# A two-layer encoder on one core: the memory branch loaded first, and the position bias made between the blocks of the first projection

## The chip, the cores and the metric

The kernel runs on one core of one Trainium2 chip. The metric is the device time of one execution in microseconds (us). The program drives TensorE (PE), VectorE (DVE), ScalarE (ACT) and GpSimd (POOL); SyncE (SP) issues every load on one queue.

## The reference, cut to what matters

256 tokens of width 1024 (`x`) and 256 memory rows of width 1024 (`mem`), all float32. Only the first stage is touched by the change; the rest (dense SwiGLU, a second layer with gated linear attention, top-2-of-8 experts, the final norm) follows it.

```python
mem_kv = rms_norm(mem, mem_norm) @ w_mem_kv          # 1024 -> 512: keys and values of 4 memory heads
u = rms_norm(x, even_norm1)
q, k, v, qm = split(u @ even_w_in)                   # 1024 -> 2560: 3 x 768 for 12 heads, 256 memory queries
mix = neighbourhood_attention(q, k, v, even_rpb)     # 12 heads, 4 x 64 grid, relative position bias, column mask
mo = softmax(qm @ mem_k.T / 8) @ mem_v               # 4 heads
h = x + concat([mix, mo]) @ even_w_out
...
```

## The kernel before

**Products in three parts.** Each float32 matrix product is made of three matmuls (`mul3`, L1288 to L1290) of a rounded high part and a low part: high by high, high by low, low by high. ACT makes the high part of each weight slot (`high_to`, L514), DVE the low part by subtraction (`low_to`, L849). A slot is 2048 columns (1 MB). `raw` holds 6 slots as loaded, `w_hi` and `w_lo` hold 3: the high part of slot n waits until the products of slot n-3 are done (`slot_done`), and the load of slot n waits until the low part of slot n-6 is made (`lo_ready`). Slots 0 and 1 are `w_mem_kv`; slots 2 to 11 are `even_w_in`, two for each block of 512 output columns (five blocks); a slot means 48 matmuls here, four output groups of twelve.

**A norm.** ACT squares and sums (`mean_squares`, L526), POOL makes 1/sqrt (L802, L805), DVE multiplies (`norm`, L864) into `xn`, PE transposes the 16 tiles (`turn`, L1309) into PSUM banks 0 to 3, and ACT and DVE cut these into `xt_hi` and `xt_lo` (`turned_high` L532, `turned_low` L870), four pieces each. `mem` is norm 0 and `x` is norm 1; both use the one buffer `gain` and the one pair `xt_hi`, `xt_lo`.

**The position bias.** `even_rpb` is loaded four times into `rp_a` at partitions 0, 32, 64 and 96 (31 rows each), two of the four shifted by one element (L418). DVE cuts it (L932, L933, L935), and 64 matmuls of 72 columns (`bias_products`, L1400) against slices of a shift matrix give, in ten groups of up to seven in banks 6 and 7, what DVE adds to a column mask (`bias_copy`, L924).

**The order by hand.** Each engine's program is written out; there is no planner. SP: tables, shifts, the four loads of the bias, `mem`, gain 0, slot 0, `x`, slots 1, 2 and 3, gain 1 (which waits until norm 0 is done), router and small tables, then the other slots. PE: bias groups 0 to 3, `turn(0)`, bias groups 4 and 5, slots 0 and 1, `turn(1)`, bias groups 6 to 9, slots 2 to 10, the scores of heads 0 and 1, slot 11, and then attention. Each block's four groups of 256 columns lie in four banks of their own, 0 to 3 and 4 to 7 in turn, and ACT (L587) and DVE (L971) copy two each.

Of the kernel before, what the change touches and what calls it, by code (L numbers as in the profile page):

```python
# [18 lines left out]
ALU = mybir.AluOpType  # L19
# [6 lines left out]
P = 128  # L26
# [103 lines left out]
def shape_constants(np):  # L130
# [13 lines left out]
    put("ident", (i == j) * 1.0)  # L144
    put("tri_f", (same & (i <= j)) / 16.0)
# [5 lines left out]
    c = np.arange(P) % GRID_W  # L151
    start = np.clip(c - 8, 0, GRID_W - 16)[:, None]
    cc = np.arange(GRID_W)[None, :]
    put("col_mask", np.where((cc >= start) & (cc < start + 16), 0.0, NEG))

# [16 lines left out]
def build(nc, col, tables, shifts, x, mem, gains, rpb, gate_aug, g_norm, router, mem_kv, even_in, even_out,  # L175
          even_gate, even_up, even_down, odd_in, odd_out, exp_gate, exp_up, exp_down, out):
    with ExitStack() as ctx:
# [18 lines left out]
        gain = sb("gain", [P, D])  # L196
        cst = sb("cst", [P, max(a + n for a, n in col.values())])
# [13 lines left out]
        rt_sb = states[:].rearrange("p d k n -> p (d k n)")[:, 0:KD * E].rearrange("p (k e) -> p k e", k=KD)  # L211
        arena = sb("arena", [P, ARENA])
# [15 lines left out]
        qkT = take(14 * T).rearrange("p (i t) -> p i t", t=T)  # L228
        v0 = take(TT * 768).rearrange("p (t n) -> p t n", t=TT)
        bias = take(NA_HEADS * NDR * GRID_W).rearrange("p (x c) -> p x c", c=GRID_W)  # L230
        s_a = take(3 * 2 * T).rearrange("p (b t m) -> p b t m", b=3, t=2)
        pT_a = take(2 * 2 * T).rearrange("p (b j q) -> p b j q", b=2, j=2)
        rp_a = take(NA_HEADS * RPB_R).rearrange("p (h r) -> p h r", r=RPB_R)
# [3 lines left out]
        mem_sb = arena[:, 0:TT * D].rearrange("p (t d) -> p t d", t=TT)  # L237
# [56 lines left out]
        def score_bank(i):  # L294

            return (0, 1, 6, 7)[i % 4] if i < 16 else 4 + i % 2
# [40 lines left out]
        def STATE_PS(d, k):  # L337
# [8 lines left out]
        tables_in, rpb_in, mem_in, x_in, gain_in = (  # L346
            sem("tables_in"), sem("rpb_in"), sem("mem_in"), sem("x_in"), sem("gain_in"))
# [47 lines left out]
        def _(sp):  # L395
# [23 lines left out]
            sp.dma_start(mem_sb, mem.rearrange("(t p) d -> p t d", p=P)).then_inc(mem_in, 16)
# [411 lines left out]
        def _(dve):  # L831
# [971 lines left out]
```

## Time and profile before

| | |
|---|---|
| median of 3 runs | 1532.38 us (1530.67 to 1533.03) |
| the profiled execution, time | 1531.72 us |
| the profiled execution, span of its instructions | 1529.9 us |
| PE, DVE, ACT busy | 96%, 77%, 64% of the span |
| mean granted clock of TensorE | 0.988 |
| first stage: up to the first product of slot 0 | 29.11 us |
| up to the first product of slot 2 | 49.08 us |
| up to the last product of slot 11 | 109.67 us |

The profile gives starts from the beginning of the span. "PEclk" is the granted clock as a share of 2.4 GHz. Idle time stands in brackets with what ended it.

### The profile page before, as it was taken

To read this page: it belongs to the slowest core of one execution; us is meant where nothing else is said; L and a number is where in the kernel's file an instruction comes from. 1 tells how busy PE (TensorE), PEld (TensorE's weight loads), DVE (VectorE), ACT (ScalarE), POOL (GpSimd) and SP (SyncE) were. 2 spreads that over 40 slices of the span, in tenths; PEclk is the share of its full clock that TensorE was granted. 3 is DMA by queue.
4 is the path that set the end of the run, shared out by engine and by line. 5 is a ranking of instruction groups with operands and counts; after the bars stand their busy time and mean duration, and the time that the engine had idled before them with its cause. 6 is when DMAs were issued, how large, how long until landed. Compare 5 with 4: busy or idle time off the path is not lost.

```text
span 1529.9 us, 20860 instructions
## 1 busy us (share of the span) xinstructions
PE 1475.2 (96%) x7832; PEld 1253.0 (82%) x7832; DVE 1173.3 (77%) x996; ACT 979.5 (64%) x909; POOL 20.5 (1%) x41
## 2 busy tenths in 40 slices
PE   5999999999998799999999999999999999999997
PEld 5985899998986688888888888888888888888885
DVE  5458554455476688898988888888889898898887
ACT  3337444333572477777777777777777777777775
POOL 1000000000001000000000000000000000000000
PEclk9999999999999899999999999999999999999999
DMA  7650465544452499999989989989999998998982
GB/s 270 229 169 1 138 208 190 175 154 138 131 193 72 161 373 383 358 324 376 380 300 386 374 311 369 381 310 377 366 354 331 384 378 303 381 374 310 370 327 93
DMA packets 198730, 428.41 MB, mean 280 GB/s; under 512 B 9533, under 2 KB 39579, under 8 KB 198684
## 3 DMA queue, kind: packets, MB, share of 16 engines
q1 hardware_dynamic: 198684, 427.79, 77.8%
q8 instruction: 30, 0.49, 0.1%
q14 instruction: 16, 0.13, 0.0%
HBM read 426.71 MB, written 1.05 MB: 280 GB/s over the span
## 4 chain that ended last, share of the span: by engine, by line
PE 89%; DVE 5%; ACT 3%; issue 2%; SPq 0%; DMA 0%; POOL 0%; DVEq 0%; POOLq 0%; ACTq 0%
PE ps L1288 27%; PE ps L1290 27%; PE ps L1289 27%; PE ps L1713 1%; DVE w_lo L1236 1%; PE ps L1682 1%; ACT w_hi L745 1%; PE ps L1389 1%; PE ps L1757 1%; PE ps L1363 1%; PE ps L1400 1%; PE ps L1309 1%; PE ps L1377 0%; DVE xt_lo L870 0%; DVE hT_lo L1247 0%
## 5 line engine op out<-in xcount | busy, mean ns | idle before, releaser
L1236 DVE TENSOR_TENSOR w_lo<-raw,w_hi 128x2048 fp32r<-128x2048 f32 (+1 forms) x224 | 442.5, 1985 | 61.5 <-ACT w_hi L745 60.7
L745 ACT ACTIVATE w_hi<-raw 128x2048 fp32r<-128x2048 f32 (+1 forms) x224 | 372.7, 1672 | 130.1 <-PE ps L1290 130.0
L1288 PE MATMUL ps<-w_hi,xt_hi 128*128 128x512 f32 (+2 forms) x1080 | 417.6, 387 | 2.4 <-DVE xt_lo L1123 1.5
L1290 PE MATMUL ps<-w_hi,xt_lo 128*128 128x512 f32 (+2 forms) x1080 | 411.1, 381 | 0.0
L1289 PE MATMUL ps<-w_lo,xt_hi 128*128 128x512 f32 (+2 forms) x1080 | 410.3, 380 | 0.0
L1236 DVE TENSOR_TENSOR w_lo<-arena,w_hi 128x2048 fp32r<-128x2048 f32 x144 | 295.6, 2053 | 29.5 <-ACT w_hi L745 28.9
L745 ACT ACTIVATE w_hi<-arena 128x2048 fp32r<-128x2048 f32 x144 | 248.6, 1726 | 82.4 <-PE ps L1290 82.1
L849 DVE TENSOR_TENSOR w_lo<-raw,w_hi 128x2048 fp32r<-128x2048 f32 (+2 forms) x69 | 149.6, 2171 | 159.3 <-ACT w_hi L514 159.2
L1288 PEld LDWEIGHTS ps<-w_hi,xt_hi 128*128 128x128 f32 x1080 | 203.1, 188 | 42.7 <-issue 3.4
L1290 PEld LDWEIGHTS ps<-w_hi,xt_lo 128*128 128x128 f32 x1080 | 203.0, 188 | 38.4
L1289 PEld LDWEIGHTS ps<-w_lo,xt_hi 128*128 128x128 f32 x1080 | 203.3, 188 | 35.0
L514 ACT ACTIVATE w_hi<-raw 128x2048 fp32r<-128x2048 f32 (+2 forms) x69 | 125.3, 1821 | 156.1 <-PE ps L1290 153.7
L1288 PE MATMUL ps<-w_hi,hT_hi 128*128 128x512 f32 x544 | 212.6, 391 | 1.8 <-DVE hT_lo L1247 1.8
L1289 PE MATMUL ps<-w_lo,hT_hi 128*128 128x512 f32 x544 | 211.8, 389 | 0.0
L1290 PE MATMUL ps<-w_hi,hT_lo 128*128 128x512 f32 x544 | 211.8, 389 | 0.0
L1288 PE MATMUL ps<-xt_hi,w_hi 128*128 128x256 f32 (+2 forms) x568 | 163.6, 288 | 4.2 <-DVE xt_lo L870 3.3
L1289 PE MATMUL ps<-xt_lo,w_hi 128*128 128x256 f32 (+2 forms) x568 | 163.3, 288 | 0.0
L1290 PE MATMUL ps<-xt_hi,w_lo 128*128 128x256 f32 (+2 forms) x568 | 163.0, 287 | 0.0
L1288 PEld LDWEIGHTS ps<-w_hi,hT_hi 128*128 128x128 f32 x544 | 102.1, 188 | 23.9 <-issue 3.3
L1290 PEld LDWEIGHTS ps<-w_hi,hT_lo 128*128 128x128 f32 x544 | 102.1, 188 | 21.5
L1289 PEld LDWEIGHTS ps<-w_lo,hT_hi 128*128 128x128 f32 x544 | 102.2, 188 | 20.5
L1288 PEld LDWEIGHTS ps<-xt_hi,w_hi 128*128 128x128 f32 (+2 forms) x568 | 108.8, 192 | 6.2 <-issue 5.6
(206 smaller groups left out, 1194.9 us busy)
## 6 DMA issues: line engine op xcount, KB each, us to landing
raw<-exp_gate SPq DMA_DIRECT2D x74, 1024.0 KB, 5.8
raw<-exp_up SPq DMA_DIRECT2D x48, 1024.0 KB, 5.6
arena<-exp_down SPq DMA_DIRECT2D x48, 1024.0 KB, 5.5
arena<-exp_up SPq DMA_DIRECT2D x40, 1024.0 KB, 7.3
raw<-exp_down SPq DMA_DIRECT2D x40, 1024.0 KB, 6.7
arena<-exp_gate SPq DMA_DIRECT2D x24, 1024.0 KB, 7.1
raw<-exp_up SPq DMA_DIRECT2D x32, 512.0 KB, 5.1
raw<-even_gate SPq DMA_DIRECT2D x11, 1024.0 KB, 5.3
```

The costliest lines, as they stand in the source:

```text
L514: act.activation(w_hi[:, n % CUT, 0:w], raw[:, n % RAW, 0:w], ACT.Copy).then_inc(hi_ready, 1)
L745: ins = act.activation(w_hi[:, n % CUT, at:at + src.shape[1]], src, ACT.Copy)
L849: dve.tensor_tensor(w_lo[:, n % CUT, 0:w], raw[:, n % RAW, 0:w], w_hi[:, n % CUT, 0:w].bitcast(F32), ALU.subtract).then_inc(lo_ready, 1)
L1236: ins = dve.tensor_tensor(w_lo[:, n % CUT, cols], src, w_hi[:, n % CUT, cols].bitcast(F32), ALU.subtract)
L1288: pe.matmul(dst, a[0], b[0], start=start, stop=False, skip_group_check=shared)
L1289: pe.matmul(dst, a[0], b[1], start=False, stop=False, skip_group_check=shared)
L1290: return pe.matmul(dst, a[1], b[0], start=False, stop=stop, skip_group_check=shared)
L1309: ins = pe.transpose(ps[:, k // 2, o:o + P], xn[:, t, P * k:P * (k + 1)], ident)
L1363: ins = pe.matmul(ps[:, score_bank(i), T * t:T * (t + 1)], q_of(i)[r, tok[t]], k_of(i)[r, :], start=True, stop=True)
L1389: ins = pe.matmul(ps[r, pair_bank(i), 0:T], v_of(i, j), pT[:, i % 2, j, :], start=(j == 0), stop=(j == 1))
L1400: ins = pe.matmul(ps[:, 6 + g % 2, 72 * cc:72 * cc + 72], shift_r[:, 63 - c:191 - c], rp_cut, start=True, stop=True)
L1682: ins = pe.matmul(ps[:, 2 + b, P * (k % 4):P * (k % 4 + 1)], xn[:, t, P * k:P * (k + 1)], pick[:, t, :], start=(t == 0), stop=(t == 1))
```

## The change

In the first stage alone:

- **Loads.** `mem` goes first. Of the tables only the first 192 columns (identity and column mask, which is moved to second place) are loaded next, with a semaphore of their own; the other columns follow slot 3. Gain 1 gets its own buffer `gain_x` and is issued after `x`, without a wait. Shifts and the position bias follow slot 1; the bias is loaded four times unshifted, and the shift is made by DVE as it cuts (seven small operations instead of three).
- **A transposed buffer for mem.** The parts of transposed `mem` go to `memT_hi` and `memT_lo`, laid over a part of the arena that is used later. PE does slot 0, then `turn(1)`, then slot 1; ACT and DVE cut transposed `x` before the copies of keys and values, and make the parts of slot 3 before these too.
- **Bias between the blocks.** The ten groups of bias matmuls stand after slots 2, 3, 4, 5 (two groups each) and 6 (groups 8 and 9). DVE's additions stand in its loop over the blocks.
- **Two banks for a block.** A block's four groups lie two to a bank, in banks 0 and 1 or 2 and 3 in turn, so that banks 6 and 7 stay free for the bias. ACT and DVE copy one whole bank (512 columns) each instead of twice 256.
- The order of the score banks is changed to match, and the waits for the rest of the tables stand after attention.

The diff, without the move of the mask's column and the names of semaphores:

```diff
@@ -209,6 +206,9 @@
...
+        with nc.sbuf_tensor("memT", [P, 2, KD, T], F32R) as memT:
+            memT_hi, memT_lo = memT[:, 0], memT[:, 1]
+        gain_x = states[:].rearrange("p d k n -> p (d k n)")[:, P:P + D]
...
@@ -225,16 +225,18 @@
...
-        qkT = take(14 * T).rearrange("p (i t) -> p i t", t=T)
...
-        bias = take(NA_HEADS * NDR * GRID_W).rearrange("p (x c) -> p x c", c=GRID_W)
...
+        mem_at = top[0]
+        assert mem_at >= 2 * KD * T
+        bias = take(NA_HEADS * NDR * GRID_W).rearrange("p (x c) -> p x c", c=GRID_W)
+        qkT = take(14 * T).rearrange("p (i t) -> p i t", t=T)
...
-        mem_sb = arena[:, 0:TT * D].rearrange("p (t d) -> p t d", t=TT)
+        mem_sb = arena[:, mem_at + NA_HEADS * NDR * GRID_W:mem_at + NA_HEADS * NDR * GRID_W + TT * D].rearrange("p (t d) -> p t d", t=TT)
...
@@ -293,7 +295,7 @@
...
-            return (0, 1, 6, 7)[i % 4] if i < 16 else 4 + i % 2
+            return (6, 7, 0, 1)[i % 4] if i < 16 else 4 + i % 2
...
@@ -405,24 +407,23 @@
...
             def next_gain(i):
-                if i >= 1:
+                if i >= 2:
...
-            sp.dma_start(cst[:], tables).then_inc(tables_in, 16)
...
-            sp.dma_start(shift, shifts).then_inc(rpb_in, 16)
-            sp.wait_ge(rp_zeroed, 1)
-            for q in (0, 64):
-                sp.dma_start(rp_a[q:q + RPB_C], rpb).then_inc(rpb_in, 16)
-                sp.dma_start(rp_a[q + 32:q + 32 + RPB_C, :, 1:RPB_R], rpb[:, :, 0:RPB_R - 1]).then_inc(rpb_in, 16)
...
+            sp.dma_start(cst[:, 0:EARLY], tables[:, 0:EARLY]).then_inc(early_in, 16)
...
+            sp.dma_start(gain_x, gains[1:2, :].partition_broadcast(P)).then_inc(gain_x_in, 16)
...
+            sp.dma_start(shift, shifts).then_inc(rpb_in, 16)
+            sp.wait_ge(rp_zeroed, 1)
+            for q in range(0, P, 32):
+                sp.dma_start(rp_a[q:q + RPB_C], rpb).then_inc(rpb_in, 16)
...
-            next_gain(1)
+            sp.dma_start(cst[:, EARLY:], tables[:, EARLY:]).then_inc(tables_in, 16)
...
@@ -529,7 +530,7 @@
...
                     act.wait_ge(turned, 4 * i + b + 1)
-                    act.activation(xt_hi[:, 2 * b:2 * b + 2, :],
+                    act.activation((memT_hi if i == 0 else xt_hi)[:, 2 * b:2 * b + 2, :],
...
@@ -563,10 +564,11 @@
...
             high_to(2)
+            turned_high(1)
+            high_to(3)
...
                 act.activation(mkT[:, b, :], ps[:, 4 + b, 0:T], ACT.Copy).then_inc(kv_copied_a, 1)
-            turned_high(1)
...
@@ -576,15 +578,14 @@
...
                     act.wait_ge(slot_done, S_IN0 + 10)
-                for i in range(2):
-                    b = 4 * ((c + 1) % 2) + i
-                    if c < 3:
-                        dst, src = qkT[:, 4 * c + i, :], ps[:, b, 0:T]
-                    elif c == 3:
-                        dst, src = v0[:, 0, 256 * i:256 * (i + 1)], ps[:, b, 0:256]
-                    else:
-                        dst, src = v0[:, i, 512:768], ps[:, b, 0:256]
-                    act.activation(dst, src, ACT.Copy).then_inc(in0_copied_a, 1)
+                src = ps[:, 2 * (c % 2), :]
+                if c < 3:
+                    dst, src = qkT[:, 4 * c:4 * c + 2, :], src.rearrange("p (i t) -> p i t", i=2)
+                elif c == 3:
+                    dst = v0[:, 0, 0:512]
+                else:
+                    dst, src = v0[:, :, 512:768], src.rearrange("p (t n) -> p t n", t=TT)
+                act.activation(dst, src, ACT.Copy).then_inc(in0_copied_a, 1)
...
@@ -856,20 +857,25 @@
...
             def norm(i, src):
-                dve.wait_ge(gain_in, 16 * (i + 1))
+                if i == 1:
+                    dve.wait_ge(gain_x_in, 16)
+                else:
+                    dve.wait_ge(gain_in, 16 * max(i, 1))
+                g = gain_x if i == 1 else gain
...
-                    dve.scalar_tensor_tensor(xn[:, t, cols], src[:, t, cols], rstd[:, k:k + 1], gain[:, cols],
+                    dve.scalar_tensor_tensor(xn[:, t, cols], src[:, t, cols], rstd[:, k:k + 1], g[:, cols],
...
-                    dve.tensor_tensor(xt_lo[:, 2 * b:2 * b + 2, :],
+                    hi, lo = (memT_hi, memT_lo) if i == 0 else (xt_hi, xt_lo)
+                    dve.tensor_tensor(lo[:, 2 * b:2 * b + 2, :],
...
-                                      xt_hi[:, 2 * b:2 * b + 2, :].bitcast(F32),
+                                      hi[:, 2 * b:2 * b + 2, :].bitcast(F32),
...
@@ -928,48 +934,61 @@
...
-            dve.wait_ge(rpb_in, 5 * 16)
-            dve.tensor_copy(rp_cut, rp_a[:, :, DR0:DR0 + NDR]).then_inc(rp_parts, 1)
-            dve.tensor_copy(shift_r, shift).then_inc(rp_parts, 1)
-            dve.wait_ge(rp_parts, 1)
-            dve.tensor_tensor(rp_cut[64:], rp_a[64:, :, DR0:DR0 + NDR], rp_cut[64:].bitcast(F32),
-                              ALU.subtract).then_inc(rp_parts, 1)
-            dve.wait_ge(tables_in, 16)
-            bias_copy(0, BIAS_A)
...
-            bias_copy(BIAS_A, BIAS_B)
...
+            turned_low(1)
+            low_to(3)
+            dve.wait_ge(rpb_in, 5 * 16)
+            for q in range(0, P, 32):
+                r0 = DR0 - q // 32 % 2
+                dve.tensor_copy(rp_cut[q:q + 32], rp_a[q:q + 32, :, r0:r0 + NDR]).then_inc(rp_parts, 1)
+            dve.tensor_copy(shift_r, shift).then_inc(rp_parts, 1)
+            for q in (64, 96):
+                r0 = DR0 - q // 32 % 2
+                dve.wait_ge(rp_parts, q // 32 + 1)
+                dve.tensor_tensor(rp_cut[q:q + 32], rp_a[q:q + 32, :, r0:r0 + NDR], rp_cut[q:q + 32].bitcast(F32),
+                                  ALU.subtract).then_inc(rp_parts, 1)
+            dve.wait_ge(early_in, 16)
...
-            for t in range(TT):
-                dve.tensor_copy(mv[:, t, :], ps[:, 6 + t, 0:256]).then_inc(kv_copied_v, 1)
-            turned_low(1)
-            bias_copy(BIAS_B, BIAS_GROUPS)
-            dve.wait_ge(router_in, 16)
-            dve.tensor_copy(rt_hi[:], rt_sb[:]).then_inc(rt_cut, 1)
-            dve.wait_ge(rt_cut, 1)
-            dve.tensor_tensor(rt_lo[:], rt_sb[:], rt_hi[:].bitcast(F32), ALU.subtract).then_inc(rt_cut, 1)
+            dve.tensor_copy(mv[:], ps[:, 6:8, 0:256]).then_inc(kv_copied_v, 1)
...
+            def in0_copy(c):
...
+                src = ps[:, 2 * (c % 2) + 1, :]
+                if c < 3:
+                    dst, src = qkT[:, 4 * c + 2:4 * c + 4, :], src.rearrange("p (i t) -> p i t", i=2)
+                elif c == 3:
+                    dst = v0[:, 1, 0:512]
+                else:
+                    dst, src = qkT[:, 12:14, :], src.rearrange("p (i t) -> p i t", i=2)
+                dve.tensor_copy(dst, src).then_inc(in0_copied_v, 1)
...
+                if c < 2:
+                    bias_copy(4 * c, 4 * c + 2)
+                if c == 2:
+                    bias_copy(8, BIAS_GROUPS)
+                if c == 3:
+                    dve.wait_ge(router_in, 16)
+                    dve.tensor_copy(rt_hi[:], rt_sb[:]).then_inc(rt_cut, 1)
+                    dve.wait_ge(rt_cut, 1)
+                    dve.tensor_tensor(rt_lo[:], rt_sb[:], rt_hi[:].bitcast(F32), ALU.subtract).then_inc(rt_cut, 1)
...
-                for i in (2, 3):
-                    b = 4 * ((c + 1) % 2) + i
-                    if c < 3:
-                        dst, src = qkT[:, 4 * c + i, :], ps[:, b, 0:T]
-                    elif c == 3:
-                        dst, src = v0[:, 1, 256 * (i - 2):256 * (i - 1)], ps[:, b, 0:256]
-                    else:
-                        dst, src = qkT[:, 12 + i - 2, :], ps[:, b, 0:T]
-                    dve.tensor_copy(dst, src).then_inc(in0_copied_v, 1)
+                in0_copy(c)
+                if c < 2:
+                    bias_copy(4 * c + 2, 4 * c + 4)
...
+            dve.wait_ge(tables_in, 16)
...
@@ -1401,48 +1420,59 @@
...
-            pe.wait_ge(tables_in, 16)
-            pe.wait_ge(rp_parts, 3)
-            bias_products(0, BIAS_A)
+            def memory_of(k, tok):
...
+                return part((memT_hi, memT_lo), k, tok)
...
+            pe.wait_ge(early_in, 16)
...
-            bias_products(BIAS_A, BIAS_B)
...
-            pe.wait_ge(bias_ready, BIAS_B)
-            project(0, [(ps[:, 4 + i, 0:T], "by feature", all_t, slice(P * i, P * (i + 1))) for i in range(2)]
-                    + [(ps[:, 6 + t, 0:256], "by token", tok[t], slice(256, 512)) for t in range(TT)], fresh=norm_halves(0))
+            kv = ([(ps[:, 4 + i, 0:T], "by feature", all_t, slice(P * i, P * (i + 1))) for i in range(2)]
+                  + [(ps[:, 6 + t, 0:256], "by token", tok[t], slice(256, 512)) for t in range(TT)])
+            project(0, kv, fresh=norm_halves(0), halves=range(1), left=memory_of)
+            pe.wait_ge(xt_lo_ready, 4)
...
-            pe.wait_ge(kv_copied_v, 2)
-            bias_products(BIAS_B, BIAS_GROUPS)
+            project(0, kv, halves=range(1, 2), left=memory_of)
...
                           else mv[:, j, HEAD * (i - 12):HEAD * (i - 11)], 0)
-            pe.wait_ge(kv_copied_a, 2)
-            pe.wait_ge(bias_ready, BIAS_GROUPS)
...
                 if c >= 2:
-                    pe.wait_ge(in0_copied_a, 2 * (c - 1))
-                    pe.wait_ge(in0_copied_v, 2 * (c - 1))
-                b = 4 * ((c + 1) % 2)
+                    pe.wait_ge(in0_copied_a, c - 1)
+                    pe.wait_ge(in0_copied_v, c - 1)
+                place = [ps[:, 2 * (c % 2) + i // 2, T * (i % 2):T * (i % 2 + 1)] for i in range(4)]
                 if c < 3:
-                    gs = [(ps[:, b + i, 0:T], "by feature", all_t, slice(P * i, P * (i + 1))) for i in range(4)]
+                    gs = [(place[i], "by feature", all_t, slice(P * i, P * (i + 1))) for i in range(4)]
...
-                    gs = [(ps[:, b + i, 0:256], "by token", tok[i // 2], slice(256 * (i % 2), 256 * (i % 2) + 256))
+                    gs = [(place[i], "by token", tok[i // 2], slice(256 * (i % 2), 256 * (i % 2) + 256))
...
                 else:
-                    gs = [(ps[:, b + t, 0:256], "by token", tok[t], slice(0, 256)) for t in range(TT)]
-                    gs += [(ps[:, b + 2 + i, 0:T], "by feature", all_t, slice(256 + P * i, 256 + P * (i + 1)))
+                    gs = [(place[t], "by token", tok[t], slice(0, 256)) for t in range(TT)]
+                    gs += [(place[2 + i], "by feature", all_t, slice(256 + P * i, 256 + P * (i + 1)))
                            for i in range(2)]
-                project(S_IN0 + 2 * c, gs, fresh=norm_halves(1) if c == 0 else None, halves=range(1) if c == 4 else range(2))
...
-            pe.wait_ge(in0_copied_a, 8)
-            pe.wait_ge(in0_copied_v, 8)
-            attention(*attention0, range(0, 2))
-            project(S_IN0 + 8, gs, halves=range(1, 2))
-            pe.wait_ge(in0_copied_a, 10)
-            pe.wait_ge(in0_copied_v, 10)
+                project(S_IN0 + 2 * c, gs, fresh=[(xt_lo_ready, 8)] * 2 if c == 0 else None, halves=range(1),
+                        second=(1, 3))
+                if c < 2:
+                    if c == 0:
+                        pe.wait_ge(kv_copied_v, 1)
+                        pe.wait_ge(rp_parts, 7)
+                    bias_products(4 * c, 4 * c + 2)
+                if c == 2:
+                    bias_products(8, BIAS_GROUPS)
+                if c == 4:
+                    pe.wait_ge(in0_copied_a, 4)
+                    pe.wait_ge(in0_copied_v, 4)
+                    pe.wait_ge(kv_copied_a, 2)
+                    pe.wait_ge(bias_ready, BIAS_GROUPS)
+                    attention(*attention0, range(0, 2))
+                project(S_IN0 + 2 * c, gs, halves=range(1, 2), second=(1, 3))
+                if c < 2:
+                    bias_products(4 * c + 2, 4 * c + 4)
+            pe.wait_ge(in0_copied_a, 5)
+            pe.wait_ge(in0_copied_v, 5)
...
+            pe.wait_ge(tables_in, 16)
```

## Rows read from the trace of the kernel before

**Rows 1.** The page, the chain that ended last: shares of the span by engine.
```profile
PE 89%; DVE 5%; ACT 3%; issue 2%; SPq 0%; DMA 0%; POOL 0%; DVEq 0%; POOLq 0%; ACTq 0%
```

**Rows 2.** Waits of the load queue from 560 to 1525: total us, times, longest.
```profile
SPq L478 <- DVE w_lo L1236: 709.0, 313, 5.4
```

**Rows 3.** Timeline of the load queue: start, us, issue.
```profile
0.73 0.40 SPq L412 DMA_DIRECT2D cst<-tables  x1
...
7.68 3.41 SPq L419 DMA_DIRECT2D arena<-mem  x1
...
11.64 0.43 SPq L400 DMA_DIRECT2D raw<-mem_kv  x1
12.11 0.83 SPq L422 DMA_DIRECT2D h<-x  x1
```

**Rows 4.** Loads of the first 16 us: KB, us from issue to landing.
```profile
h<-x SPq DMA_DIRECT2D x1, 1024.0 KB, 11.0
...
cst<-tables SPq DMA_DIRECT2D x1, 480.0 KB, 3.5
```

**Rows 5.** Loads of the first 12 us, rate in 40 slices of 0.3 us.
```profile
GB/s 0 0 0 0 0 64 51 77 256 422 435 358 268 43 24 22 20 8 8 8 8 8 8 8 8 15 22 2 5 24 15 8 8 8 8 8 8 8 8 221
...
arena<-mem SPq DMA_DIRECT2D x1, 1024.0 KB, 7.9
raw<-mem_kv SPq DMA_DIRECT2D x1, 1024.0 KB, 9.0
```

**Rows 6.** Timeline of ACT: start, us, operation.
```profile
15.62 0.63 ACT L526 ACTIVATE xn<-arena 128x512 f32<-128x512 f32 x1 [13.60 <-DMA arena<-mem]
...
20.62 1.91 ACT L514 ACTIVATE w_hi<-raw 128x2048 fp32r<-128x2048 f32 x1 [2.44 <-DMA raw<-mem_kv]
22.98 2.06 ACT L532 ACTIVATE xt_hi<-ps 128x512 fp32r<-128x512 f32 x4 [0.44 <-PE ps L1309]
```

**Rows 7.** Timeline of POOL.
```profile
17.53 0.57 POOL L805 TENSOR_TENSOR rstd<-ss,mhalf 128x1 f32<-128x1 f32 x1
```

**Rows 8.** Timeline of DVE.
```profile
19.75 2.73 DVE L864 SCALAR_TENSOR_TENSOR xn<-arena,rstd,gain 128x512 f32<-128x512 f32 x4
22.57 2.29 DVE L849 TENSOR_TENSOR w_lo<-raw,w_hi 128x2048 fp32r<-128x2048 f32 x1
25.59 0.68 DVE L924 TENSOR_TENSOR arena<-ps,cst 128x504 f32<-128x504 f32 x1 [0.73 <-PE ps L1400]
...
27.69 2.47 DVE L870 TENSOR_TENSOR xt_lo<-ps,xt_hi 128x512 fp32r<-128x512 f32 x4
...
66.68 0.74 DVE L971 COPY arena<-ps 128x256 f32<-128x256 f32 x2
```

**Rows 9.** Timeline of PE.
```profile
12.95 6.16 PE L1400 MATMUL ps<-hT_lo,hT_hi 128*128 128x72 f32 x28 [12.95 <-DVE hT_lo L935]
20.55 3.67 PE L1309 MATMUL ps<-cst,xn 128*128 128x128 f32 x16 [1.44 <-DVE xn L864]
...
29.11 0.55 PE L1288 MATMUL ps<-xt_hi,w_hi 128*128 128x256 f32 x1 [2.06 <-DVE xt_lo L870]
...
42.05 1.91 PE L1309 MATMUL ps<-cst,xn 128*128 128x128 f32 x16
43.71 1.73 PE L1400 MATMUL ps<-hT_lo,hT_hi 128*128 128x72 f32 x14
47.10 1.08 PE L1400 MATMUL ps<-hT_lo,hT_hi 128*128 128x72 f32 x8 [1.65 <-DVE arena L924]
...
110.61 1.14 PE L1363 MATMUL ps<-arena 64*128 64x256 f32 x8 [0.94 <-DVE arena L971]
```

**Rows 10.** Stretches: us, busy us (instructions) by engine, granted clock, DMA share, GB/s.
```profile
49.08:52.60 3.52, 3.52 (x17) 3.52 (x18) 3.52 (x3) 0.00 (x0) 0.00 (x0) 0.52 0.08 8
49.08:102.50 53.42, 53.42 (x432) 53.37 (x432) 25.61 (x19) 17.50 (x16) 0.00 (x0) 0.97 0.56 188
...
175.00:176.00 1.00, 0.27 (x2) 0.28 (x3) 1.00 (x2) 0.00 (x0) 0.83 (x2) 0.77 1.02 422
```

More of the change, by code:

```diff
@@ L144, in shape_constants @@
     put("ident", (i == j) * 1.0)
+    c = np.arange(P) % GRID_W
+    start = np.clip(c - 8, 0, GRID_W - 16)[:, None]
+    cc = np.arange(GRID_W)[None, :]
+    put("col_mask", np.where((cc >= start) & (cc < start + 16), 0.0, NEG))
     put("tri_f", (same & (i <= j)) / 16.0)
@@ L150, in shape_constants @@
     put("iota", np.broadcast_to(np.arange(P), (P, P)))
[L151 to L154, printed above, removed]
     x, dc = np.arange(SHIFT_W)[None, :], np.arange(RPB_C)[:, None]
@@ L196, in build @@
         gain = sb("gain", [P, D])
+        EARLY = P + GRID_W
         cst = sb("cst", [P, max(a + n for a, n in col.values())])
@@ L345, in build @@
         hi_ready, lo_ready, slot_done = sem("hi_ready"), sem("lo_ready"), sem("slot_done")
-        tables_in, rpb_in, mem_in, x_in, gain_in = (
-            sem("tables_in"), sem("rpb_in"), sem("mem_in"), sem("x_in"), sem("gain_in"))
+        tables_in, rpb_in, mem_in, x_in, gain_in, gain_x_in, early_in = (
+            sem("tables_in"), sem("rpb_in"), sem("mem_in"), sem("x_in"), sem("gain_in"), sem("gain_x_in"), sem("early_in"))
         gnorm_in, router_in, gate_w_in, stored = (
```

## Prediction

> **What bounds the kernel now.** I read the page first, for the chain that ended last: PE has 89% of it, no DMA at all [rows 1]. So time is gained only where PE starts earlier, does less, or works at a higher clock. Next, whether a gain in the first stage can be lost later. In the expert stage the load queue waited 709.0 us for low parts of weights [rows 2]: loads wait for the engines, not the engines for loads. That stage begins later and runs as long; a shift of the first stage passes through whole.
>
> Then the timelines of the first stage. PE's first matmul is at 12.95, its first product of slot 0 at 29.11, and it reaches attention at 110.61 after 0.94 us of waiting, so its last product ends at 109.67 [rows 9]. In front of 29.11 PE does 42 bias matmuls and 16 transposes at 1.2 GHz: 28 matmuls take 6.16 us, against 1.73 us for 14 later [rows 9]. What PE waits for at the start is the load queue. `mem` is issued at 7.68 [rows 3] and lands 7.9 us later, at 15.58 [rows 5, 6]; the rate shows why: from 4.2 to 11.7 us the queue moves 8 to 25 GB/s, against about 400 in full flow [rows 5]. Those are the four bias loads. From 29.11 to 109.67 PE has only short holes, so that stretch is worth its count of matmuls.
>
> **The start, step by step.** `mem` takes the place of the tables: issued at 0.73; the tables' 480 KB land 3.5 us later [rows 3, 4]. One MB more costs 2.55 us (slot 0 lands at 11.64+9.0=20.64, `x` at 12.11+11.0=23.11, rounded with the wait in rows 6 that ends at 20.62) [rows 3 to 6]. 544 KB more than the tables are 1.4 us: `mem` lands at 5.6. A gain and slot 0 came 5.0 us behind `mem` (15.58 to 20.6) [rows 6]; the early tables, 96 KB, add an estimated 0.4: slot 0 lands at 11.0, `x` at 13.5, gain 1 and slot 1 again 5.0 later, at 18.5. A gain is thus taken at 2.4 us for 512 KB; at the rate of `x` it would be 1.3, so slot 1 could land up to 2.2 us earlier. That is the lower bound.
>
> Norm 0 isn't late: 1/sqrt of the first tokens was ready at 18.10, 2.5 us after `mem` landed [rows 6, 7]; now at 8.1, norm until 10.9 (2.73 us [rows 8]), transposes until 12.7. Slot 0 then decides: high part 1.91 us, low part 2.29, and the first two of four low pieces of transposed `mem` 1.25 (half of 2.47) plus 0.15 [rows 6, 8], so 5.6 after landing: PE's first product of slot 0 is at 16.6, where it was at 29.11.
>
> Slot 0 is 48 products of 0.12 us: (53.42-1.5)/432, where 1.5 is what 17 products at a granted clock of 0.52 cost more (3.52 less 17 x 0.12) [rows 10]. PE is cold again here, so 5.8+1.4=7.2 us: until 23.8. Slot 1 lands at 18.5: high 20.4, low 22.7, norm 1 until 25.4, last transposes 26.1. In that time PE has only the 16 transposes. Slot 1 follows until 31.9.
>
> The second path to slot 2 goes through the queue: behind slot 1 stand the shifts (96 KB, 0.4) and four plain bias loads. Before, each load without the shift moved at 20 to 24 GB/s for 0.9 us, each shifted one at 8 for 2.6 us [rows 5]. Now all four are plain: 4 x 0.9 = 3.6. Bounds: 7.0, if nothing of the slow stretch goes away, and 0.2, if they run beside the large ones. I take 3.6, the price of the same shape. On the Trainium skill (DMA: Bandwidth & Descriptors, section "Why a DMA increments its semaphore by 16 and not by 1") a transfer runs on the largest number of engines up to 16 that divides its outer size; 31 rows are prime, so one engine takes each. The rate of 20 to 24 GB/s agrees with one of sixteen; by that rule too it is 3.6, and 0.2 is excluded.
>
> Slot 2 lands at 18.5+0.4+3.6+2.6=25.1. High part until 27.0; only then does ACT cut transposed `x` (2.06), until 29.1; DVE's four low pieces, behind the low part of slot 2 (29.3), end at 31.8 [rows 6, 8]. PE needs all four. Both paths thus end at 31.8 to 31.9; for a tie of two I add 0.3 and take 32.2 for the first product of slot 2.
>
> **From slot 2 to slot 11.** 480 products x 0.12 = 57.7. The 64 bias matmuls are now between products at 2.4 GHz: 14 took 1.73, so 7.8 for all [rows 9]. Scores of heads 0 and 1: 1.1 [rows 9]. Together 66.6: the last product ends at 98.8, against 109.67, 10.9 earlier. Before, the same work took 57.7 + 1.5 + 1.1; the bias has moved in and costs 7.8 here, where it had stood ahead. The DVE copy after slot 11 is one of 512 columns in place of two of 256: 0.68 by rows of that width against 0.74 [rows 8], gain 0.06, left out.
>
> **What costs nothing, and its cover.** The bias additions (ten of 0.68) and cuts (seven small operations, some 1.4 us) are on DVE. In order: before the copy of values DVE makes the low part of slot 3 (34.1) and the cuts (35.5); PE asks for both at the end of slot 2, 38.0, cover 2 us. Afterwards each addition stands behind the low part of a later slot, whose high part waits for a slot to end: 1.9+2.3, a copy 0.7, two additions 1.4, so 6.3 us after the end of slot n, while PE asks after its two groups and slot n+1, 1.7+5.8=7.5. Cover 1.2 us, at slots 3, 4 and 5; behind a late addition PE's bias matmuls and all products wait, microsecond for microsecond. ACT, with one copy of 0.6, is never late. Two banks in turn instead of four: the block after next waits for copies that end 5 us or more before. The rest of the tables follows slot 3 (1.0 us more for slot 4, which lands at about 32 and is wanted at 47); it is needed after attention. Gain 1's wait (0.7 us on DVE before) goes. Score banks in another order, `memT` laid over later space, and mask columns moved: same operations.
>
> **The rivals.**
>
> *A. As worked out*: 10.9 less. The profiled execution's 1531.72 lies 0.66 under the median of the runs and 1.8 over its own span; I take the difference from the median: 1532.38-10.9=1521.5.
>
> *B. A later start of slot 2.* Either the bias loads cost 7.0 (slot 2 lands 3.4 later, each microsecond counts): 1524.9. Or the clock falls around `turn(1)`, where PE has 2.3 us with transposes only. For it: after 2.22 us without a matmul the clock went to 0.77 in 175 to 176, then 0.50 [rows 10]. Against: through the 16 transposes at 42.05, 1.91 us at full speed, and the bias matmuls after them, 1.73, it held; it was low only from 49.08 [rows 9, 10]. Price 1.5: 1523.0. Both: 1526.4. The Trainium skill (TensorE: Matmul & The Clock Gate, "Part 4: PE-mode transpose") says that transposes don't count as busy for the gate; by it the gap is empty and 1523.0 is the result. The transposes at 42.05 neither confirm nor refute that, since the clock held through them.
>
> *C. DVE is late for the bias.* The cover of 1.2 us at three places is used up if its operations take a fifth longer beside each other; 1 us lost at each gives 1524.5. Against: the low part and cuts before took the same 2.29 wherever they stood.
>
> *D. Slower.* The bias matmuls between the slots (72 columns, a weight load each) keep the clock at half for the projection. A product then costs 0.21 instead of 0.12 (3.52/17 [rows 10]); 480 of them are 43 us, so 1564. It decides from 10.9/0.09=120 products on, two and a half slots. For it: the fall at 49.08 came after bias matmuls and two holes. Against: 14 of them ran in 1.73, and if it fell after each of the five places for 3.5 us, that is 7.5 in all, still 1529.0.
>
> *E. The start doesn't count.* Slot 0 is not sooner because another load holds it, or the gain is eaten by a later stage: 1532. Against: rows 2 and the 7 slow microseconds in rows 5.
>
> *F. More than worked out.* Gains at the speed of `x` and bias loads beside others: slot 1 lands at 16.3, 2.2 earlier, 13.1 in all: 1519.3.
>
> **How the numbers follow.** A 0.64, B 0.17, C 0.05, D 0.03, E 0.04, F 0.07. The likeliest is A, 1521.5. The range takes in A, B with both parts nearly, C and F: 1519 to 1526; D, E and the ends of B and F stay out. A measurement of this kernel can tell about 0.2%, 3.1 us, from no change. A, B, C and F are beyond it: faster 0.93. E: same 0.04. D: slower 0.03.
>
> **What the profile after would show.** `mem` landing near 5.6 and the first squares there; the first product of slot 0 at 16.6; transposes of `x` between 23.8 and 26.1; slot 2 at 32.2; bias matmuls about 0.12 us apart without a DVE wait before them; attention's first wait ending at 99.7. Wrong would be: slots 0 or 1 landing late (a slower gain or many loads at once), slot 2 landing beyond 25.5, a granted clock under 1 after 27, or PE waiting for L924. If the first product of slot 2 is right and attention is late, the bias between the blocks was priced too low; if attention is 11 us earlier and the time is not, the loss is in a later stage.

## Result and profile after

The changed kernel takes 1520.42 us (median of 4 runs, 1519.72 to 1521.01) against 1532.59 of the kernel before in the same comparison: 12.2 us less, ratio 0.9925 with a 95% interval from 0.9913 to 0.9937. A second measurement, told below, gave 1522.38 us, ratio 0.994 (0.9928 to 0.9953), 9.1 us less. The forecast was 10.9 less.

The page of the changed kernel: span, PE's share, granted clock by slice.

```profile
span 1519.2 us, 20854 instructions
...
PE 1471.8 (97%) x7832; PEld 1248.3 (82%) x7832; DVE 1173.6 (77%) x994; ACT 979.4 (64%) x904; POOL 21.2 (1%) x41
...
PEclk9999999999999899999999999999999999999999
```

Its timeline of ACT, to be laid beside [rows 6]: `mem`, slot 0, slot 1 and slot 2 land where the bracket names a load.

```profile
5.66 0.63 ACT L527 ACTIVATE xn<-arena 128x512 f32<-128x512 f32 x1 [3.64 <-DMA arena<-mem]
...
10.87 1.91 ACT L515 ACTIVATE w_hi<-raw 128x2048 fp32r<-128x2048 f32 x1 [2.66 <-DMA raw<-mem_kv]
...
17.42 1.91 ACT L515 ACTIVATE w_hi<-raw 128x2048 fp32r<-128x2048 f32 x1 [0.25 <-DMA raw<-mem_kv]
24.91 1.91 ACT L515 ACTIVATE w_hi<-raw 128x2048 fp32r<-128x2048 f32 x1 [5.58 <-DMA raw<-even_in]
26.73 2.04 ACT L533 ACTIVATE xt_hi<-ps 128x512 fp32r<-128x512 f32 x4
```

DVE, norm 1, the low parts of `x`, and the additions for bias groups 2 and 3:

```profile
21.58 2.73 DVE L869 SCALAR_TENSOR_TENSOR xn<-h,rstd,states 128x512 f32<-128x512 f32 x4
...
29.07 2.48 DVE L876 TENSOR_TENSOR xt_lo<-ps,xt_hi 128x512 fp32r<-128x512 f32 x4
...
49.93 1.26 DVE L930 TENSOR_TENSOR arena<-ps,cst 128x504 f32<-128x504 f32 x2
```

And PE, beside [rows 9]. L1328 are the transposes, L1307 the first of three products, L1419 the bias, L1382 the scores.

```profile
9.13 3.75 PE L1328 MATMUL ps<-cst,xn 128*128 128x128 f32 x16 [9.13 <-DVE xn L869]
16.45 0.55 PE L1307 MATMUL ps<-memT,w_hi 128*128 128x256 f32 x1 [3.56 <-DVE memT L876]
...
24.43 1.91 PE L1328 MATMUL ps<-cst,xn 128*128 128x128 f32 x16
...
31.83 0.28 PE L1307 MATMUL ps<-xt_hi,w_hi 128*128 128x256 f32 x1
...
37.58 1.65 PE L1419 MATMUL ps<-hT_lo,hT_hi 128*128 128x72 f32 x14
...
52.20 1.65 PE L1419 MATMUL ps<-hT_lo,hT_hi 128*128 128x72 f32 x14
...
66.82 0.98 PE L1419 MATMUL ps<-hT_lo,hT_hi 128*128 128x72 f32 x8
...
90.84 1.14 PE L1382 MATMUL ps<-arena 64*128 64x256 f32 x8
98.81 1.14 PE L1382 MATMUL ps<-arena 64*128 64x256 f32 x8 [0.88 <-DVE arena L968]
```

What the reader is to see: between 16.45 and 98.81-0.88=97.93 no row of PE has a bracket, so PE waits for nothing. Two stretches, with the count of products in each (columns as in [rows 10]):

```profile
16.45:21.60 5.15, 5.15 (x24) 5.15 (x25) 3.29 (x4) 2.63 (x5) 1.41 (x3) 1.00 0.79 253
31.90:97.93 66.03, 66.03 (x553) 65.33 (x552) 36.44 (x38) 22.84 (x20) 0.00 (x0) 1.00 0.66 230
```

The first has 24 products in 5.15 us, 0.21 each: 1.2 GHz. (The clock column reads 1.00 for it, as it does for the first stretches of the kernel before; here the spacing of the products tells the level.) The second, from slot 2 to slot 11 with the bias inside, runs at 2.4 GHz throughout.

The last product of slot 11, the "stage end" from here on, moves from 109.67 to 97.93, 11.7 us. Slot 2 starts 17.3 us earlier than before (31.83 against 49.08), and the stretch behind it is 5.5 us longer, since the bias stands in it. The spans differ by 10.7. The remainder of the program, from stage end to the end of the span, is 1420.2 before and 1421.3 after. The place can be named: the transposes of norm 2 start at 163.94 (175.73 before, 11.8 sooner), those of norm 3 at 358.13 (368.24 before, 10.1 sooner). In between the work is the same, and the granted clock is low for longer behind norm 2: 0.63 in 164 to 168 and 0.52 in 168 to 172, where before it was 0.63 in 176 to 180 and 1.00 from 180 on.

```profile
163.94 1.45 PE L1328 MATMUL ps<-cst,xn 128*128 128x128 f32 x8 [2.22 <-DVE xn L869]
...
358.13 1.32 PE L1328 MATMUL ps<-cst,xn 128*128 128x128 f32 x8 [1.44 <-DVE xn L869]
```

```profile
164.00:168.00 4.00, 3.34 (x16) 2.37 (x17) 2.80 (x5) 1.46 (x4) 1.92 (x4) 0.63 0.21 85
168.00:172.00 4.00, 3.99 (x19) 4.00 (x20) 3.22 (x4) 2.40 (x3) 0.00 (x0) 0.52 0.01 4
```

This loss is not tied to the change: from the transposes of norm 2 to those of norm 3 it is 192.3 to 192.5 us in nine of the thirteen kernels profiled here (the one before among them) and 194.2 to 194.4 in four (the changed kernel twice, loads first, bias rows split).

### The profile page after: what moved, and what is told of

Same layout as the page of the kernel before. It is cut to its first block, busy times and chain, and to the rows that moved or that the text cites. A ratio compares the mean times of both kernels' runs of the same rounds, so it can differ in the third digit from the quotient of the medians.

```text
span 1519.2 us, 20854 instructions
## 1 busy us (share of the span) xinstructions
PE 1471.8 (97%) x7832; PEld 1248.3 (82%) x7832; DVE 1173.6 (77%) x994; ACT 979.4 (64%) x904; POOL 21.2 (1%) x41
## 4 chain that ended last, share of the span: by engine, by line
PE 90%; DVE 4%; ACT 3%; issue 2%; DMA 1%; POOL 0%; SPq 0%; DVEq 0%; POOLq 0%; ACTq 0%
PE ps L1307 27%; PE ps L1309 27%; PE ps L1308 27%; PE ps L1743 1%; DVE w_lo L1255 1%; PE ps L1712 1%; ACT w_hi L746 1%; PE ps L1408 1%; PE ps L1787 1%; PE ps L1382 1%; DMA raw<-mem_kv 1%; PE ps L1396 0%; PE ps L1419 0%; PE ps L1680 0%; PE ps L1627 0%
## 5 line engine op out<-in xcount | busy, mean ns | idle before, releaser
L1307 PE MATMUL ps<-w_hi,xt_hi 128*128 128x512 f32 (+2 forms) x1064 | 413.4, 389 | 2.6 <-DVE xt_lo L1142 1.5
L1309 PE MATMUL ps<-w_hi,xt_lo 128*128 128x512 f32 (+2 forms) x1064 | 407.0, 383 | 0.0
L1308 PE MATMUL ps<-w_lo,xt_hi 128*128 128x512 f32 (+2 forms) x1064 | 406.1, 382 | 0.0
L1307 PEld LDWEIGHTS ps<-w_hi,xt_hi 128*128 128x128 f32 x1064 | 200.1, 188 | 42.6 <-DVE w_lo L1255 3.6
L1307 PE MATMUL ps<-w_hi,hT_hi 128*128 128x512 f32 x544 | 212.8, 391 | 1.8 <-DVE hT_lo L1266 1.8
L1307 PE MATMUL ps<-xt_hi,w_hi 128*128 128x256 f32 (+2 forms) x552 | 158.0, 286 | 1.0 <-DVE xt_lo L876 1.0
L1308 PE MATMUL ps<-xt_lo,w_hi 128*128 128x256 f32 (+2 forms) x552 | 157.5, 285 | 0.0
L1309 PE MATMUL ps<-xt_hi,w_lo 128*128 128x256 f32 (+2 forms) x552 | 157.4, 285 | 0.0
L1307 PEld LDWEIGHTS ps<-w_hi,hT_hi 128*128 128x128 f32 x544 | 102.2, 188 | 23.9 <-issue 3.3
L1307 PEld LDWEIGHTS ps<-xt_hi,w_hi 128*128 128x128 f32 (+2 forms) x552 | 104.6, 190 | 2.9 <-issue 2.3
```

The costliest lines, as they stand in the source:

```text
L1307: pe.matmul(dst, a[0], b[0], start=start, stop=False, skip_group_check=shared)
L1308: pe.matmul(dst, a[0], b[1], start=False, stop=False, skip_group_check=shared)
L1309: return pe.matmul(dst, a[1], b[0], start=False, stop=stop, skip_group_check=shared)
```

## Experiments

All are read by stage end from one profile each, since the rest of the program varies by more than some of the differences. The medians come from four comparisons, each with its own kernel before (1532.59; 1532.15 for experiments 1, 2, 4 and 5; 1531.40 for 6, warm and combined; 1531.43 for 3, combined shorter and changed again), so the ratios are what can be compared between rows. Expectations stand as recorded.

| kernel | stage end | against changed | median us | ratio to before (95%) |
|---|---|---|---|---|
| before | 109.67 | +11.7 | 1532.59 | 1 |
| changed | 97.93 | | 1520.42 | 0.9925 (0.9913 to 0.9937) |
| changed, again | 98.02 | +0.1 | 1522.38 | 0.994 (0.9928 to 0.9953) |
| loads first | 102.53 | +4.6 | 1525.66 | 0.9958 (0.9941 to 0.9974) |
| bias block ahead of slot 2 | 106.52 | +8.6 | 1529.32 | 0.999 (0.9977 to 1.0003) |
| bias block behind slot 2 | 103.28 | +5.4 | 1525.4 | 0.9959 (0.9945 to 0.9973) |
| one transposed buffer | 103.00 | +5.1 | 1528.06 | 0.998 (0.9965 to 0.9995) |
| before, mem first | 110.78 | +12.9 | 1534.28 | 1.0019 (1.0009 to 1.0028) |
| bias loads late | 96.96 | -1.0 | 1519.69 | 0.9928 (0.9913 to 0.9942) |
| bias rows split | 98.11 | +0.2 | 1521.86 | 0.9938 (0.9924 to 0.9953) |
| warm PE | 97.86 | -0.1 | 1523.73 | 0.9947 (0.9933 to 0.9961) |
| combined | 96.28 | -1.7 | 1520.48 | 0.9943 (0.9929 to 0.9957) |
| combined, shorter | 95.66 | -2.3 | 1518.03 | 0.9917 (0.9904 to 0.993) |

**1. The order of the loads undone** (u_loads). The order of issue, in short form:

```diff
-mem, tables[:, 0:EARLY], gain 0, slot 0, x, gain_x, slot 1, shifts, 4 x rpb, slots 2 and 3, tables[:, EARLY:]
+tables[:, 0:EARLY], tables[:, EARLY:], shifts, 4 x rpb, mem, gain 0, slot 0, x, gain_x, slot 1, slots 2 and 3
```

> Theory (the start is set by when slot 0 lands, and from its first product on PE never waits): tables, shifts and the four plain bias loads ahead of mem cost 1.2+0.4+3.6 us, so mem lands near 11.2 instead of 5.7, the first product of slot 0 is near 21.9 instead of 16.45, and the last product of slot 11 ends near 103.4 instead of 97.9: 1525.9 us. Rival (the start doesn't set the time, the order of PE's work does): 1520.4 as the changed kernel.

Two rows, of ACT and of PE:

```profile
12.40 0.63 ACT L527 ACTIVATE xn<-arena 128x512 f32<-128x512 f32 x1 [10.39 <-DMA arena<-mem]
```

```profile
21.96 0.36 PE L1307 MATMUL ps<-memT,w_hi 128*128 128x256 f32 x1 [2.35 <-DVE memT L876]
...
103.41 1.14 PE L1382 MATMUL ps<-arena 64*128 64x256 f32 x8 [0.88 <-DVE arena L968]
```

`mem` is 6.7 us later where 5.5 was expected, slot 0's first product 5.5 as expected, the stage end 4.6. What stands ahead of `mem` cost more than the 5.2 us it was given, but slot 0 landed only 5.5 later (its high part at 16.38, against 10.87), so this was hidden. The theory holds, and the rival falls: the queue sets the start. Of the 5.5 about 0.7 comes back because the cold stretch at slot 0 is shorter here (transposes at 29.21, 7.25 us after slot 0's first product, against 7.98).

**2. The bias in one block ahead of slot 2** (u_bias).

```diff
+            pe.wait_ge(kv_copied_v, 1)
+            pe.wait_ge(rp_parts, 7)
+            bias_products(0, BIAS_GROUPS)
             for c in range(5):
...
-                    bias_products(4 * c, 4 * c + 2)
...
-                    bias_products(4 * c + 2, 4 * c + 4)
```

DVE does cuts, the copy of values and all ten additions ahead of the low part of slot 3. This is not the place that the bias had in the kernel before (in three parts, two of them ahead of slot 0): it tests one block against five.

> Theory (between the blocks the bias costs only its matmuls, 7 us; in one block PE also waits for DVE): DVE ends the low parts of x at 31.6, cuts and the copy of values until 33.9, then ten groups at a pace of 0.85 us, so the first product of slot 2 is near 42.4. Against 31.9 and 7.0 later that is 3.5 us lost, 5.0 if the clock falls in the block: 1523.9 to 1525.4. Rival (the place of the bias is worth nothing, DVE keeps up in the block): the first product of slot 2 near 39 and 1520.4.

The block in PE's timeline, and its stretches with the clock:

```profile
33.81 12.63 PE L1415 MATMUL ps<-hT_lo,hT_hi 128*128 128x72 f32 x64 [1.87 <-DVE mv L956]
```

```profile
33.81:38.00 4.19, 4.19 (x26) 4.19 (x26) 2.05 (x3) 1.49 (x1) 0.00 (x0) 0.68 1.05 385
38.00:42.00 4.00, 4.00 (x21) 4.00 (x20) 1.58 (x3) 0.00 (x0) 0.00 (x0) 0.50 0.82 304
```

The direction was right, the size was not: 8.6 us lost where at most 5.0 were expected. The block took 12.63 us instead of 8.5, because the clock was at 1.2 GHz from about 35 on, and slot 2 began cold: it was granted half until about 48.9. The median, 1529.32, is 3.9 above the upper bound of 1525.4.

**3. The same block where PE does not wait before it** (bias_block_inside): all ten groups behind slot 2, DVE's additions behind the low part of slot 4.

> The changed kernel with all ten bias groups in one block behind slot 2, where PE does not wait before them. Theory (in the block ahead of slot 2 the clock fell because of the 1.9 us without a matmul, the two-bank pace of 0.91 us a group at full clock is the rest): block of 8.5 to 9 us at full clock, stage end 1.5 to 2 us later than the changed kernel's 97.9. Rival (72-column matmuls in turn with DVE don't hold the clock by themselves): it falls inside the block, pace 1.49 us a group, stage end 5 to 8 us later.

```profile
37.75 10.04 PE L1415 MATMUL ps<-hT_lo,hT_hi 128*128 128x72 f32 x64
```

```profile
37.60:42.00 4.40, 4.40 (x39) 4.18 (x37) 3.46 (x5) 1.91 (x1) 0.00 (x0) 1.00 1.05 387
42.00:46.00 4.00, 4.00 (x23) 3.90 (x22) 2.05 (x3) 0.00 (x0) 0.00 (x0) 0.59 1.04 381
46.00:50.00 4.00, 4.00 (x20) 4.00 (x20) 3.06 (x4) 0.00 (x0) 0.00 (x0) 0.50 0.20 75
```

My theory fell: no gap stood before this block, and still the clock went to half inside it, near 42.7, 5 us after its start. The stage ended 5.4 later, within the rival's 5 to 8: 2.7 of it is the block (10.0 us instead of 7.3), and most of the rest the products behind it, at half clock until about 52.9. So a long run of 72-column matmuls in turn with DVE does not hold 2.4 GHz here, while five runs of at most 14, each between slots of 48 products, do (66.03 us at 1.00 above). PE hardly waited for DVE while the clock was full: an addition every 0.87 us (four between 38.65 and 42.14), against 0.82 us for seven matmuls without DVE (1.65 for 14). Whether the short matmuls alone bring the clock down, or the small pauses with them, no run here separates. It is the prediction's case D as a mechanism; the change avoids it by where it puts the groups.

**4. One transposed buffer for mem and x** (u_shared_xt): `memT` replaced by `xt_hi` and `xt_lo`, and

```diff
             high_to(2)
+            act.wait_ge(slot_done, 2)
             turned_high(1)
```

with the same wait on DVE ahead of `turned_low(1)`.

> Theory (memT lets the cut of x run under slot 1): with one buffer ACT and DVE wait until slot 1 is done at 31.9; four high parts and the last low part take 3.0, so slot 2 starts near 35.0: 3.1 us lost, up to 4.6 if the clock falls in the empty 3 us: 1523.5 to 1525.0. Rival (the buffer is not needed, since slot 2's low part is late anyway): no more than 0.3 us lost.

```profile
35.55 0.55 PE L1309 MATMUL ps<-xt_hi,w_hi 128*128 128x256 f32 x1 [3.37 <-DVE xt_lo L877]
```

Slot 2 starts at 35.55, 3.7 later than in the changed kernel, after 3.37 us of waiting. Then its first products are cold, 1.4 more: the first bias group is at 42.65 instead of 37.58, 5.1 later, and the stage end too, 0.5 more than the 4.6 expected at most. The buffer is needed. The median, 1528.06, lies 3.1 above the recorded 1525.0; the last section shows where such a difference comes from.

**5. The kernel before with mem first and nothing else** (mem_first_alone).

> The kernel before with mem moved to the head of the queue and nothing else. Theory (mem first is worth something only if the bias is not first on PE and DVE): mem lands near 5.6, but the bias loads 2.6 us later, the first bias matmul is near 15.6, slot 0 lands at 20.6 as before, and the norm of mem still stands behind four additions: 2.3 to 2.6 us slower than before, near 1535. Rival (mem was what the start waited for): the first product of slot 0 up to 7 us sooner, near 1526.

The squares start at 5.74, but the bias has moved to 15.68 and the first product of slot 0 to 30.30 (29.11 before). Stage end 1.1 later, ratio 1.0019. In this profile it is slower by less than expected, because two bias groups behind the first transposes ran at full clock (1.73 us instead of the 3.18 of before). The profiled run, 1532.89, is the second shortest of ten; their median, 1534.28, is 2.1 us above the kernel before, near the 2.3 to 2.6 expected. Loading `mem` first is worth nothing while PE and DVE begin with the bias.

**6. What stands in front of slot 2** (late_bias, split_rows).

```diff
 # late_bias: shifts and the four bias loads behind slots 2 and 3
 # split_rows (DVE's wait counts nine loads instead of five):
-                sp.dma_start(rp_a[q:q + RPB_C], rpb).then_inc(rpb_in, 16)
+                sp.dma_start(rp_a[q:q + 16], rpb[0:16]).then_inc(rpb_in, 16)
+                sp.dma_start(rp_a[q + 16:q + RPB_C], rpb[16:RPB_C]).then_inc(rpb_in, 16)
```

> The changed kernel with shifts and bias loads behind slots 2 and 3. Theory (PE goes from slot 1 into slot 2 without a wait, so the bias loads in front of slot 2 are hidden): the high part of slot 2 starts near 20.5 instead of 24.9, the first product of slot 2 stays at 31.9, time 1520.4 within 0.5. Rival (the landing of slot 2 sets its first product): up to 1 us less in the stage.

> The changed kernel with each bias load of 31 rows split into one of 16 and one of 15 rows. Theory (a load of 31 rows runs on one DMA engine of the 16, and the loads behind it wait for that one): the four take well under 1 us together, slot 2's high part starts near 21 instead of 24.9; the time stays at 1520.4, since this wait is hidden. Rival (short rows are slow as such, or each load costs a fixed time): the high part starts at 24.9 or later.

The high part of slot 2, first with the bias loads late, then with the rows split:

```profile
20.17 1.92 ACT L515 ACTIVATE w_hi<-raw 128x2048 fp32r<-128x2048 f32 x1 [0.80 <-DMA raw<-even_in]
```

```profile
21.59 1.92 ACT L516 ACTIVATE w_hi<-raw 128x2048 fp32r<-128x2048 f32 x1 [2.21 <-DMA raw<-even_in]
```

Against 24.91, shifts and bias loads cost slot 2 4.7 us as they are, and 1.4 with the rows split into 16 and 15, shifts included. By the Trainium skill (DMA: Bandwidth & Descriptors, "Why a DMA increments its semaphore by 16 and not by 1") 31 rows go to one engine; this pair agrees, 4.7 against 1.4 us for the same bytes. With split rows an earlier slot 2 by 3.3 us gave a stage end 0.2 later, since PE was then the later path, and its cold stretch at slot 0 was 0.4 longer (transposes of `x` at 24.80). With late loads the first product of slot 2 did not stay at 31.9, as the theory had it, but came at 30.85, and the stage ended 1.0 sooner, as the rival had it. 0.8 of this is a shorter cold stretch of slot 0 (transposes of `x` at 23.65, 7.16 us after its first product, against 7.98). That gain needed the earlier landing too: in the warm kernel below PE was 0.7 sooner with the landing unchanged, and slot 2 started only 0.15 sooner. So the loads ahead of slot 2 are hidden by a hair, behind a path of PE that is as long: shortening either alone gains next to nothing, both together gain.

**7. A warm PE, and a version better than both** (warm, combined, combined_short): `idle_work(n)` issues n matmuls of the identity by itself into bank 7, where nobody reads the result.

```diff
             pe.wait_ge(early_in, 16)
+            idle_work(12)
             turn(0)
+            idle_work(24)    # 17 in combined_short
```

The combined kernels also have the late bias loads and, on DVE, `norm(1, h)` ahead of `low_to(1)`.

> The changed kernel with 12 matmuls of no use ahead of the transposes of mem and 24 behind them, in bank 7. Theory (slot 0 runs its first 5 us at 1.2 GHz because PE had been idle): the clock is at 2.4 GHz when slot 0 starts at 16.5, slot 0 ends near 22.2 instead of 24.5; norm 1 ends at 24.3 and the low parts of x at 31.6, so slot 2 starts near 31.7 and only 0.2 to 0.3 us are won. Rival (the cold stretch is worth its full 2 us): slot 2 near 29.8, 1518.4.

> The changed kernel with the useless matmuls, the bias loads behind slot 3, and norm 1 ahead of the low part of slot 1. Theory (behind the cold clock stand norm 1 and the landing of slot 2, each hidden so far): norm 1 18.4 to 21.1, low part of slot 1 until 23.4, slot 1 from 23.9, slot 2 from 29.7: 2.2 us less than the changed kernel, 1518.2. Rival (the matmuls of no use don't lift the clock, since transposes and gaps lie between): 1520.4 or slower by what they delay.

> As the combined kernel, with 17 matmuls of no use behind the transposes instead of 24. Theory (each counts as two, 0.115 us apart, and in the combined kernel they held slot 0 back from 16.5 to 17.4): slot 0 starts at 16.5 to 16.6, stage end 95.4 to 95.6, 0.8 less than the combined kernel and 2.4 less than the changed one. Rival (the start is not set by that): 96.3 again.

> The changed kernel itself, beside the others: stage end 97.1 to 98.1, by how long slot 0 runs at 1.2 GHz; 1519.5 to 1521.5 us. It tells how far the same program varies behind the stage.

Warm PE alone, then the shorter combination:

```profile
12.93 5.52 PE L1429 MATMUL ps<-cst 128*128 128x128 f32 x48
23.77 1.91 PE L1328 MATMUL ps<-cst,xn 128*128 128x128 f32 x16
31.68 0.36 PE L1307 MATMUL ps<-xt_hi,w_hi 128*128 128x256 f32 x1 [0.54 <-DVE xt_lo L876]
```

```profile
12.89 3.96 PE L1429 MATMUL ps<-cst 128*128 128x128 f32 x34
22.35 1.91 PE L1328 MATMUL ps<-cst,xn 128*128 128x128 f32 x16
...
96.54 1.14 PE L1382 MATMUL ps<-arena 64*128 64x256 f32 x8 [0.88 <-DVE arena L968]
```

Warm alone: the useless matmuls ran 0.115 us apart, at full clock, but two for each call, until 18.45, and held slot 0 back, from 16.45 to 18.21; slot 2 then waited 0.54 us for the low parts of `x`, at 31.68. So an earlier end of slot 0 by itself buys 0.15 us there (0.2 to 0.3 expected); the rival, slot 2 near 29.8, falls. Combined, with 24 matmuls behind the transposes, slot 0 still starts late, at 17.40, slot 2 at 30.17 where 29.7 was expected, and the stage ends at 96.28, 1.7 sooner instead of 2.2. Its median, 1520.48, is the rival's 1520.4, but not for the rival's reason: the clock was up, and the time was lost behind the stage (last section). With fewer of them, slot 0 starts at 16.61 and is through at 22.35 instead of 24.43, and the stage ends at 95.66, 2.3 before the changed kernel. Its median is 1518.03 against 1522.38 of the changed kernel in the same comparison; the two intervals of the ratio (0.9904 to 0.993, 0.9928 to 0.9953) just meet, so the stage is shown to be shorter and the whole time very likely so. The changed kernel repeated had its stage end as expected (98.02), but its median is 0.9 above the 1521.5 expected at most: behind the stage the same program varies by more than was thought.

## Why the prediction was right

- *Loads pass the start's delay on.* `mem` at 5.66 (forecast 5.6), slot 0 at 10.87 (11.0), slot 0's first product at 16.45 (16.6). Experiment 1 shows it as a cause.
- *Slot 1.* It landed at 17.4, not 18.5: a gain and a slot behind `x` cost 4.0 us here, not the 5.0 taken from before. Norm 1 ended at 24.3 (25.4). That was the part of the lower bound that I had left in the range.
- *Slot 0's cold stretch.* 24 products at 0.21 us, not 15 to 17: slot 0 ended at 24.43 (23.8). So PE, not norm 1, set the transposes of `x`, and these errors offset each other: the transposes ended at 26.09 (26.1), slot 2 started at 31.83 (32.2). That is luck.
- *Bias loads.* 4.7 us with the shifts, not 4.0; with the earlier slot 1, slot 2 was ready at 24.9 (25.1): two errors of 1.1 and 0.7 us against each other, luck again. Two paths were said to tie, and they did: the one through PE decided (31.83) by 0.15 to 0.3 us over the low parts of `x` (ready at 31.55; PE started 31.68 in the warm kernel, where it waited for them). The 0.3 us added for the tie was not spent.
- *The bias between the blocks.* 66.1 us from slot 2 to the stage end (forecast 66.6): 57.7 and 1.1 as said, 7.3 for the bias instead of 7.8. No wait for DVE. Case C did not occur: the additions for groups 2 and 3 ended at 51.2 (1.26 us from 49.93), the groups that need them began at 52.20, a cover of 1.0 us where 1.2 was worked out.
- *Stage end* 97.93 (98.8), 11.7 sooner instead of 10.9. On the whole time 12.2 in one comparison and 9.1 in the other: the forecast lies between. That a shift of the stage passes through whole was right for the load queue, and not for the clock: in the profile 1.1 of the 11.7 us was lost behind the stage.
- *Case B* did not occur: through `turn(1)`, 1.91 us of transposes between slots 0 and 1, the clock held. The sentence of the Trainium skill (TensorE: Matmul & The Clock Gate, "Part 4: PE-mode transpose") that would have made the gap empty gave the wrong time for this place; whether transposes count is not settled by it.
- *Case F* could not come at its price. By the prediction's own numbers slot 0 holds PE until 23.8, so with slot 1 2.2 us sooner the transposes could end at about 25.5 instead of 26.1, and slot 2 gain 0.6, not 2.2. Slot 1 was 1.1 sooner, and almost nothing of it arrived.
- *Case D* was argued away too lightly. It did not occur in the change, but experiments 2 and 3 show its mechanism at 5 to 9 us when the same 64 matmuls stand together.
- *Small slips.* One MB costs 2.47 us by the rows (23.11 less 20.64), not 2.55; the slow stretch of rows 5 moves 2 to 24 GB/s, not 8 to 25; 64 times 1.73/14 is 7.9, not 7.8. None moves the forecast by more than 0.2 us.

The three parts undone singly cost 4.6, 8.6 (or 5.4) and 5.1, more together than the 11.7 that all gave: each needs the others. (Undone means a variant of the changed kernel, not the old order in every detail; two banks for a block, the seven cuts and the buffer for gain 1 were not tried by themselves.) With the bias first, an early `mem` is useless (experiment 5); with one buffer or a block, PE idles or cools where it now runs through.

## What to carry to other kernels

Order the head of a load queue by what the first chain of work needs, and count what narrow loads do to the loads behind them, not their bytes. Moving a load pays only if the work that uses it is also first on every engine that it passes. Small matmuls that alternate with another engine are best put between long runs of large ones: in one block they lost the clock here, 5.4 us even where PE did not wait before the block. And where two paths end together, look for both before shortening one.

## What the runs showed of the hardware that was not expected

- The same program differs behind the stage by its clock. The kernel with one transposed buffer ran ten times: five runs in 1524.2 to 1525.7 with a mean granted clock of 0.986 to 0.989, five in 1530.5 to 1533.5 with 0.980 to 0.982. The profile of the warm kernel shows where such a difference can lie: its attention stage, whose order of work is the same in all of these kernels, ran at half clock.

```profile
100.00:110.00 10.00, 8.79 (x27) 4.89 (x28) 7.87 (x24) 5.93 (x19) 0.00 (x0) 0.66 0.00 0
110.00:120.00 10.00, 10.00 (x26) 5.27 (x24) 4.80 (x14) 3.65 (x11) 0.00 (x0) 0.50 0.00 0
```

  In the changed kernel both stretches were at 1.00, with 40 and 47 matmuls instead of 27 and 26. From stage end to the end of the span the warm kernel took 1427.7 us, the others 1419.4 to 1422.1. From stage end to the transposes of norm 2, with attention in between, it is 66.0 to 66.1 us in ten of the thirteen profiles, 67.3 in two (bias loads late, combined; granted clock 0.53 and 0.50 in 102 to 104) and 73.7 in the warm kernel. PE waits for DVE 0.88, 0.88 and 0.39 us at the start of this stage in the changed kernel too, whose clock held. So the late loads had lost by norm 2 the 1.0 us that they had won in the stage. A second such place is behind norm 2, told with the result (1.9 us). What decides was not tried and stays open. It is also why medians of kernels that differ by 1 or 2 us in the stage can stand in the wrong order.
- The cold stretch at slot 0 lasted between 7.2 and 8.4 us from slot 0's first product to the transposes in kernels with the same work there, a difference of up to 1.2 us.
